# Splits between the decay chain's steps, a down tile ahead of the last turns, raw residual for the memory queries, memory turns around a tile

## What is computed

```python
# first layer
h = rms_norm(x, g0)
q, k, v, r, a_lr = split(h @ w_in)                 # 1024, 1024, 2048, 2048, 16
log_a = log_sigmoid(a_lr @ w_a2 + b_a) / 16        # the decay; summed along time
...                                                # scores with the decay between two tokens
x = x + (rms_norm(o, g_norm) * silu(r)) @ w_out
g, u = split(rms_norm(x, g1) @ w_gu)
x = x + (silu(g) * u) @ w_down
# second layer
h = x + concat(o_nsa, o_sb) @ w_out_2
q = rmsnorm(h, norm_mem_q) @ w_q                   # memory attention
k, v = rmsnorm(mem, norm_mem_kv) @ w_k, ... @ w_v
h = h + (softmax(q @ k.T * scale) @ v) @ w_o
h = h + peer_ffn(rmsnorm(h, norm_ffn), ...)        # 8 heads, 16 of 16384 experts each
out = rmsnorm(h, norm_final)
```

## Time and profile before

| | us |
|---|---|
| three runs | 3134.68, 3143.16, 3144.44 |
| median | 3143.16 |
| profiled execution | 3140.97 |
| its span, first to last instruction | 3139.1 |
| PE busy | 2751.3 (88% of the span) |
| DVE busy | 2113.9 (67%) |
| ACT busy | 1148.5 (37%) |
| POOL busy | 985.0 (31%) |

### The profile page before, as it was taken

How to read it: one execution, slowest core, us unless ns; L and a number is a source line. 1 busy time by engine, 2 the same in 40 slices (tenths; PEclk the granted TensorE clock), 3 DMA queues, 4 the chain that set the end, 5 groups by cost and what they waited for, 6 DMA issues and landing times.

```text
span 3139.1 us, 34650 instructions
## 1 busy us (share of the span) xinstructions
PE 2751.3 (88%) x12196; PEld 1993.0 (63%) x12196; DVE 2113.9 (67%) x2872; ACT 1148.5 (37%) x1982; POOL 985.0 (31%) x566
## 2 busy tenths in 40 slices
PE   8999999999999999999989994666767777679997
PEld 7888788888887888999778892222223343235433
DVE  5587565555564555445555569888788888779877
ACT  5455555555553335445655541000002330034000
POOL 0011000000000000000000007877778877778864
PEclk9999999999999999989999996888898888978999
DMA  6444445555554554443334449999999999999997
GB/s 250 155 161 148 174 179 187 189 192 189 188 187 170 187 187 171 162 170 126 134 138 171 163 175 398 403 416 415 410 419 410 418 410 405 408 397 369 409 403 305
DMA packets 123586, 827.89 MB, mean 264 GB/s; under 512 B 22167, under 2 KB 22183, under 8 KB 23855
## 3 DMA queue, kind: packets, MB, share of 16 engines
q0 software_dynamic: 79392, 510.36, 40.1%
q1 hardware_dynamic: 43920, 313.73, 27.6%
q10 hardware_dynamic: 144, 2.10, 0.2%
HBM read 892.00 MB, written 4.22 MB: 285 GB/s over the span
## 4 chain that ended last, share of the span: by engine, by line
PE 20%; POOL 13%; DVE 9%; DMA 8%; issue 4%; ACT 2%; DVEq 0%; ACTq 0%
POOL rows L1296 13%; PE ps L598 11%; DMA rows<-peer_u,arena 5%; PE ps L1203 3%; DVE arena L2402 3%; PE ps L1214 2%; DMA rows<-peer_v 2%; DMA rows<-peer_v,arena 1%; PE ps L1194 1%; DVE arena L209 1%; DVE arena L202 0%; ACT arena L1762 0%; DVE arena L203 0%; DVE arena L206 0%; DVE arena L199 0%
## 5 line engine op out<-in xcount | busy, mean ns | idle before, releaser
L503 DVE SCALAR_TENSOR_TENSOR WL<-ring,PA,WH 128x512 fp32r<-128x512 f32 x896 | 632.5, 752 | 473.9 <-ACT WH L486 458.6
L1214 PE MATMUL ps<-rows,rstd 128*128 128x512 f32 x1164 | 638.8, 703 | 289.6 <-DMA rows<-peer_v,arena 203.6
L2402 DVE CUSTOM_DVE_ANT_0 arena<-rows,arena 128x2048 f32<-128x2048 f32 x256 | 586.9, 2293 | 140.9 <-DMA rows<-peer_u,arena 111.7
L1214 PEld LDWEIGHTS ps<-rows,rstd 128*128 128x128 f32 x1164 | 250.0, 224 | 664.9 <-issue 383.0
L1296 POOL DMA_INDIRECT rows<-peer_v,arena x256 | 483.2, 1888 | 197.2 <-DVE arena L2402 72.9
L485 ACT ACTIVATE WH<-ring,PA 128x512 fp32r<-128x512 f32 x448 | 324.0, 723 | 547.1 <-PE ps L598 395.9
L1296 POOL DMA_INDIRECT rows<-peer_u,arena x256 | 449.4, 1756 | 167.2 <-DVE WL L503 82.2
L598 PE MATMUL ps<-WH,HH 128*128 128x512 f32 x1120 | 443.3, 396 | 8.6 <-DVE WL L503 6.2
L598 PE MATMUL ps<-WH,HL 128*128 128x512 f32 x1120 | 438.6, 392 | 0.0
L598 PE MATMUL ps<-WL,HH 128*128 128x512 f32 x1120 | 438.5, 391 | 0.0
L598 PE MATMUL ps<-HH,WH 128*128 128x256 f32 x1088 | 312.3, 287 | 21.1 <-DVE WL L503 21.1
(11 more groups left out here) (361 smaller groups left out, 3574.5 us busy)
## 6 DMA issues: line engine op xcount, KB each, us to landing
ring<-stream SPq DMA_DIRECT2D x292, 1024.0 KB, 4.8
rows<-peer_v POOLq DMA_DIRECT2D x32, 1024.0 KB, 15.6
rows<-peer_u,arena POOLq DMA_INDIRECT x256, 14.1
rows<-peer_v,arena POOLq DMA_INDIRECT x256, 14.3
arena<-xT SPq DMA_DIRECT2D x4, 512.0 KB, 8.9
bias_rows<-bias_scratch POOLq DMA_DIRECT2D x1, 2048.0 KB, 12.6
arena<-xT ACTq DMA_DIRECT2D x1, 2048.0 KB, 10.8
arena<-memT POOLq DMA_DIRECT2D x1, 2048.0 KB, 9.1
```

Of the source, the lines that this page charges most:

```text
L503: ins = nc.vector.scalar_tensor_tensor(out=half_tile(WL, u)[:, s], in0=raw_half(u)[:, s], scalar=gain[d], in1=half_tile(WH, u).bitcast(f32 ...
L1214: last = mm(ps[:, 4 * tt + q, :], DIAG[:, k % DIAGS, :], rows[:, SLOTS[n % ROWS], q * CH:(q + 1) * CH], start=n == mine[0], stop=n == ends[q])
L2402: ins = V.tensor_tensor_reduce(out=JUNK, in0=rows[:, SLOTS[n % ROWS], :], in1=HN[:, tt, :], scale=1.0, scalar=0.0, op0=ALU.mult, op1=ALU.a ...
```

## The change

It has seven parts.

1. Opening: PE multiplies one tile of chunk 1 between the fourth and the fifth turn; DVE copies the bias row behind `W.until(8)` in place of ahead of it.
2. Decay chain: ACT rounds unit 36 ahead of exp and unit 37 ahead of ln, DVE splits two units ahead of its step behind ln, one in the middle of the running sums and one behind the clearing, and both do the units up to tile 20 ahead of the first level's exp and product.
3. Down: half of the first down tile's products (four of its eight blocks, in banks 0, 1, 6 and 7) come ahead of the last `turn_act`, the other half behind it.
4. Memory turns: PE multiplies the seventh out2 tile between the fourth and the fifth turn; ACT squares ahead of making `MNH`, with two splits between the fourth and the fifth square and two more ahead of `MNH`.
5. Statistics: DVE does its splits up to tile 12 of out2 ahead of the wait for the memory's statistics.
6. Raw residual for the memory queries: `chunk_by_tile`, the two `norm_tile` and `xhat` calls of "norm3" and `add_tile` go. The last chunk is an ordinary one, `turn_raw` turns the residual, and the queries' 1/rms goes with the softmax scale into `MEM_SCALE`, by which the exp and the maximum of the memory logits are scaled. ACT and DVE do the splits up to tile 16 of out2 (four units beyond it) ahead of the last addition and the squares.
7. Experts: `choose(0, units=2)` has one split behind each of its two top-16 searches.

The diff, cut to its core:

```diff
@@ PE @@
             for j in range(8):
                 tt, q = j // 4, j % 4
+                if j == 4:
+                    chunk(1, T_GLA_IN + 4, XX, "T", part=(0, 1))
...
-            chunk(1, T_GLA_IN + 4, XX, "T")
+            chunk(1, T_GLA_IN + 4, XX, "T", part=(1, 4))
...
-            turn_act(N_GU - 1)
...
+            early = [(free, m, 0) for m in range(2)] + [(1, m, 1) for m in range(2)]
+            for d, m, s in early:
+                down_block(0, 2 * T_DOWN + d, m, s, first=True)
+            turn_act(N_GU - 1)
...
-            chunk(c + 1, T_OUT2 + 4, XX, "N", part=(3, 4))
             pe.wait_ge(sem("mem_in"), 16)
             for j in range(8):
                 tt, q = j // 4, j % 4
+                if j == 4:
+                    chunk(c + 1, T_OUT2 + 4, XX, "N", part=(3, 4))
...
-            chunk_by_tile(c + 3, T_OUT2 + 12, XX, opened=True)
+            chunk(c + 3, T_OUT2 + 12, XX, "N", part=(2, 4))
...
-            turn_first("norm3", banks)
+            turn_raw("norm3", 0)
+            turn_raw("norm3", 1)
             chunk(c, T_MEM, (MNH, MNL), "T", part=(2, 4), ready=("raw_split", 9))
-            turn_second("norm3", banks)
+            turn_raw("norm3", 2)
+            turn_raw("norm3", 3)
@@ POOL @@
-            pool.wait_ge(sem("residual_added"), 13)
+            pool.wait_ge(sem("residual_added"), 12)
@@ ACT @@
+            W.units_to(2 * 16 + UNITS + 1)
             act.wait_ge(sem("z_abs"), 1)
             flat = E.rearrange("p a b -> p (a b)")
             ch.link(A(flat, flat, ACT.Exp, scale=-1.0))
+            W.units_to(2 * 16 + UNITS + 2)
             ch.mark(A(flat, flat, ACT.Ln, bias=1.0), "z_ln")
             W.until(18)
...
+            W.until(20)
             level_exp(1)
...
             for j in range(8):
+                if j % 4 == 0:
+                    W.until(T_OUT2 + 7 + j // 4)
...
+            W.until(T_OUT2 + 9)
+            for g in range(4):
+                A(MNH[:, 4 * g:4 * g + 4, :], ML[:, 4 * g:4 * g + 4, :], ACT.Copy).then_inc(sem("raw_leading"), 1)
...
-                act.wait_ge(sem("residual_added"), 4 + n + 1)
-                for tt in range(TT):
-                    square_part("norm3", tt, n)
-            W.until(T_OUT2 + 14)
-            for tt in range(TT):
...
+                raw_squares("norm3", n)
+            W.until(T_OUT2 + 16)
+            raw_squares("norm3", 3)
+            raw_roots("norm3")
@@ DVE @@
+                if name == "norm3":
+                    ch.link(V.tensor_scalar(MEM_SCALE, RSTD[name], ATT_SCALE, None, ALU.mult))
...
+            W.until(8)
             dve.wait_ge(sem("bias_mm"), 1)
...
-            W.until(8)
...
+            W.units_to(2 * 16 + UNITS + 2)
             dve.wait_ge(sem("z_ln"), 1)
...
             for j in range(8):
+                if j == 4:
+                    W.units_to(2 * 18 + UNITS + 1)
...
             ch.mark(V.memset(QP, 0.0), "decayed_cleared")
+            W.units_to(2 * 18 + UNITS + 2)
...
             level_diff(1)
+            W.until(20)
...
+            W.until(T_OUT2 + 12)
             dve.wait_ge(sem("stat_rows"), 2)
             ch.mark(V.tensor_copy(RBM, ps[:, 4, 0:TOK]), "stat_rows_read")
             add_chunk(c, T_OUT2, 2, 4)
-            W.until(T_OUT2 + 14)
-            dve.wait_ge(sem("first_tile"), 1)
-            add_tile(c + 3, 0)
-            W.unit()
-            norm_tile("norm3", 0)
...
+            add_chunk(c, T_OUT2, 3, 4)
+            raw_norm("norm3")
...
-            choose(0)
+            choose(0, units=2)
```

99 lines of the change are left out of this document (35 added, 64 removed).

## The result

The changed kernel takes **3106.3 us** (median of four runs, 3102.4 to 3109.6) against 3143.8 for the kernel before on the same chip. The ratio is 0.9886, with a 95% interval from 0.9864 to 0.9909: faster by 37 us, or 1.1%. The forecast was 3108.

The account below looks back on a forecast made before the run. TensorE's weight stream was taken to bound the kernel up to DVE's first gathered row, the row gathering after it. Terms 4.2 + 7.7 + 4.2 + 15.5 + 2.2 = 33.8 us gave 3107.2 to 3109.4, stated as 3108; range 3099 to 3124.

Parts of the forecast that it names:

- the gathering gives it back: Rival, row stage: it has its own end, not tied to DVE's start, all 33.8 us lost; 3136 to 3142, chance 0.07.
- the slower one: Rival, decay levels: DVE's backlog does not shrink and each of nine levels stops TensorE; 3153 us, chance 0.03.
- Opening: Second turns and bias row at the start: waits for ScalarE's squares and the bias copy go, gain 4.2 us.
- Decay chain: Exp, ln and scans: two TensorE waits and their clock loss go, a new wait of 1.2 to 2.0 comes; gain 7.7 us.
- Less 0.8 in which four splits took 6.20 instead of 5.39 beside a POOL product: Decay chain, DVE's way to unit 44: 0.8 us subtracted for splits slowed beside POOL's product.
- the locked port: Rival, decay chain: DVE loses POOL's whole 2.35 us, not 0.81; term 5.4, time 3110, chance 0.08.
- they lost a third of it: Argument against the locked port: splits beside POOL's product of 2.35 us lost only 0.81 us.
- Less the 3.56 it stood idle: Decay chain, DVE's way to unit 44: 3.56 us of idle time subtracted from 35.5, toward 28.4 us.
- First down tile: Pauses around the last turns: twelve matmuls fill the first pause, 2.8 us plus half the clock loss; gain 4.2 us.
- Memory turns and raw residual: Memory stage to the residual's last chunk: 13.2 us idle and 4.1 clock, 17.3, taken as 15.5 for the tight order.
- Choice of experts: First choice on DVE: two splits inside it remove TensorE's wait of 2.16 us; gain 2.2 us.
- DVE late in part: Rival: decay term falls to 5 or less, memory term keeps only 9; 3117 to 3124 us, chance 0.18.

Follow-up runs that it names:

- the four kernels with this order and the same 3.7 us at the logits: The changed kernel without its memory turns, raw residual, opening, or split in the experts, one left out in each: 3118.3, 3111.4, 3107.1 and 3107.3 us.
- the kernel with four splits first: Changed kernel, but DVE splits units 44 and 45 ahead of the sum, 46 and 47 ahead of the second level's difference: 3107.9 us.
- the kernel without the splits: The changed kernel without its second part, no splits between the steps of the decay chain: 3108.1 us.

## Why the prediction was right, and where it was wrong

**The ground held.** TensorE's stream sets when DVE reaches the gathered rows, and these carry the gain to the end: 1853.64 against the 1855 named, and 1252.8 us behind it against 1250.3. The rival that the gathering gives it back falls, and so does the slower one: behind 182 no level stops TensorE in the changed kernel.

**Opening, 4.2 forecast, 4.4 to 4.6 measured.** Both waits went and nothing came in their place.

**Decay chain, 7.7 forecast, 2.4 to 2.7 measured** (4.1 to 4.3 if before is held against the four kernels with this order and the same 3.7 us at the logits). Of the 5.0 that are missing in the execution after, 2.3 are idle time: 6.2 - 2.0 = 4.2 was counted, and TensorE's idle time fell by 1.9. The other 2.7 are clock: 3.5 was counted, and its busy time fell by 0.8. This term failed in four steps. (1) "Less 0.8 in which four splits took 6.20 instead of 5.39 beside a POOL product": the loss was compared with the length of the product. It should have been compared with the overlap. In the earlier trace rows the product ends at 157.20 + 2.35 = 159.55, and the splits start at 158.54: they overlap for 1.0 us and lose 0.8 of it. That was the locked port already; the argument "they lost a third of it" read the same rows the wrong way round. The new order puts splits under the whole product twice, and each time 2.1 us go. The rival named this and priced it for the first product, with a wait of 3.6 us at unit 44 and a term of 5.4. The wait was 2.56, and behind it TensorE did not stop again in the execution after, although the second product cost DVE as much. The rule of the Trainium skill, SBUF — State Buffer, section "Who interferes with whom", was right here, by the 2.89 us of one split and by the row at 174.64 of the kernel with four splits first, whose one tensor input lies in PSUM and which took its usual 0.69 us beside a POOL product. (2) "Less the 3.56 it stood idle": 0.57 us of idle time stayed, between the difference and the next split. With 28.4 + 0.57 + 2.14 = 31.1 us the same sum gives DVE's way from the step behind ln to unit 44 as measured: from 136.52 to 167.70, just ahead of TensorE's start at 167.74, it is 31.2. (3) The three early waits, 0.77, 0.54 and 0.45 us, were not in the sum at all: "every split of those two fours has its own place in the chain" was taken to mean that each would be in time. (4) The clock: 1.7 and 2.8 us were counted as if the waits caused them for certain, and the 2.8 was itself misread ("14 x 0.2", where a clock of 0.77 gives 14.09 x 0.23 = 3.2). In the kernel without the splits the second wait cost none. And the long stretch of lower clock at the logits in the execution after, 5.13 us instead of 3.69, took 1.4 away at a place that the change does not touch.

The table loads cost what the trace said. ScalarE's timeline after:

```profile
128.63 1.28 ACT L1348 ACT_TABLE_LOAD   x1
129.93 1.92 ACT L1348 ACTIVATE arena<-arena 128x2048 f32<-128x2048 f32 x1
```

The rounding ahead of the load ends at 128.61 (127.90 + 0.71), the load at 129.91, and the exp starts 0.02 us behind it. The drain of 1.38 us that the Trainium skill, ScalarE: Activation LUTs, section "What ACT_TABLE_LOAD costs", adds does not show here on either side.

**First down tile, 4.2 forecast, 4.1 to 5.5 measured.** 2.85 us of idle time, as counted. The clock gave 2.7 between the two profiled executions and 1.3 when the part was left out; "I count half" was a fair guess for something that chance decides.

**Memory turns and raw residual, 15.5 forecast, 18.5 measured.** The waits were 13.2 and are all gone; the discount from 17.3 to 15.5 for a tight order had no ground. The rest, 5.3, is clock, where 4.1 were counted.

**Choice of experts, 2.2 forecast, 2.4 measured,** and 3.9 when left out, with 1.7 of clock.

So the total was right within 2 us because a term that was 5.0 too high met others that were 4.9 too low, and 1.5 came between the stages. That they cancelled was luck; the path, the places of the waits and most of the idle time were understood, the clock and the decay chain were not. (The text speaks of ten waits; its parts name eleven, and the 0.84 behind the last turns.) The range, 3099 to 3124, was wider than this needed on the side that did not come. "DVE late in part" came true in its first half (the decay term under 5) and not in its second.

## What to carry to other kernels

Lay the long two-input DVE instructions and POOL's products side by side in the timeline and compare the loss with their overlap: here it was nearly the whole overlap, and moving DVE's splits under POOL's product cost 2.1 us each time. When splits are moved ahead of a chain, keep one for every step that the engine will wait for; spending them all early made a wait of 5.1 us out of one of 2.6. Count the idle time that an edit removes only after a look at which engine is late next (of the 4.2 us counted in the decay chain 1.9 were gained, of those elsewhere all), count the lower clock behind it as a chance, and read small parts from the distance between two instructions, not from the median.
